# Fewer copies of a bias row in DRAM, low parts of a split operand on one engine, and doubled queries for the first pairs of an attention stage

## What is computed

```
def project(x, W):
    p = rmsnorm(x, W['norm_mix']) @ W['w_in']        # one projection for all head groups
    q, kv, gate, z, xbc, dt_raw = split(p)
    q = rmsnorm(q, W['q_norm'])                      # 8 query heads of 64, 2 KV heads
    ...
bias = rel_bias[rel_bucket(q_pos - k_pos)]           # added to the logits of every branch
def attend_shared(q, q_pos, k, v, k_pos, mask, rel_bias):
    s = einsum('...qgrd,...kgd->...qgrk', q, k) * HEAD_DIM ** -0.5
    p = masked_softmax(s + bias, mask)
    return einsum('...qgrk,...kgd->...qgrd', p, v), p
```

## Time and profile before

| | us |
|---|---|
| median of 3 runs | 2066.74 (2059.92 to 2070.21) |
| profiled execution, its own time | 2045.3 |
| span of its trace | 2043.5 |
| PE busy | 1868.7 (91%) |
| DVE, ACT, POOL busy | 827.5, 741.3, 374.5 |

### The profile page before, as it was taken

One profiled execution on the slowest core, in us unless ns is written; L12 is line 12 of the kernel. 1 busy time (PEld: TensorE's weight loads), 2 busy tenths in 40 slices (PEclk: granted clock), 3 DMA queues, 4 the chain that ended last, 5 costly groups with the idle time before them and its releaser, 6 DMA issues. The chain is left out here.

```text
span 2043.5 us, 31118 instructions
## 1 busy us (share of the span) xinstructions
PE 1868.7 (91%) x11797; PEld 1531.7 (75%) x11797; DVE 827.5 (40%) x1809; ACT 741.3 (36%) x1534; POOL 374.5 (18%) x429
## 2 busy tenths in 40 slices
PE   6879997999988886998986987999999999799899
PEld 5878996666655564655654867999999999587686
DVE  6431266666664573456363442111111211433532
ACT  5222542576664142355352542111111110432422
POOL 5221111343332435325250000000000000000000
PEclk9989997799996897999997998999999999899999
DMA  5543130110000018548394212112111110401300
GB/s 141 83 126 97 42 95 16 40 35 12 12 13 1 1 24 304 170 144 288 124 331 157 75 65 83 41 41 60 43 41 41 50 53 1 134 31 55 119 34 23
DMA packets 155352, 165.93 MB, mean 81 GB/s; under 512 B 45502, under 2 KB 121831, under 8 KB 155178
## 3 DMA queue, kind: packets, MB, share of 16 engines
q1 hardware_dynamic: 136498, 96.81, 16.9%
q0 software_dynamic: 18432, 67.12, 9.4%
q10 hardware_dynamic: 312, 0.52, 0.1%
HBM read 144.37 MB, written 18.47 MB: 80 GB/s over the span
## 5 line engine op out<-in xcount | busy, mean ns | idle before, releaser
L2630 PE MATMUL banks<-u_parts,w_parts 128*128 128x352 f32 x3168 | 505.4, 322 | 8.9 <-DVE w_parts L2644 8.9
L2630 PEld LDWEIGHTS banks<-u_parts,w_parts 128*128 128x128 f32 x3168 | 505.1, 188 | 9.0 <-issue 9.0
L2776 PE MATMUL banks<-w_down_hi,g_parts 128*128 128x512 f32 (+1 forms) x792 | 250.4, 394 | 19.2 <-DVE g_parts L2800 19.2
L467 PE MATMUL banks<-u_parts_mix,w_in_parts 128*128 128x352 f32 x1440 | 246.2, 329 | 21.6 <-ACT columns L631 15.7
L467 PEld LDWEIGHTS banks<-u_parts_mix,w_in_parts 128*128 128x128 f32 x1440 | 232.9, 190 | 25.3 <-ACT columns L631 15.9
L2652 DVE TENSOR_TENSOR gT<-silu_gate,banks 128x352 f32 (+1 forms) x66 | 34.4, 521 | 417.6 <-PE banks L2630 417.6
L2776 PEld LDWEIGHTS banks<-w_down_hi,g_parts 128*128 128x128 f32 (+1 forms) x792 | 142.9, 180 | 63.6 <-DVE w_down_lo_b L2797 20.0
L2800 DVE TENSOR_TENSOR g_parts<-gT,g_parts 128x256 fp32r<-128x256 f32 (+1 forms) x198 | 77.9, 402 | 156.4 <-ACT g_parts L2759 156.4
L2084 ACT ACTIVATE turned<-banks 128x512 f32<-128x512 f32 (+1 forms) x136 | 78.9, 590 | 164.6 <-PE banks L1949 164.1
L1961 PE MATMUL banks<-turned,cmp_w 128*128 128x512 f32 x256 | 134.0, 606 | 4.3 <-DVE turned L2086 2.4
L2759 ACT ACTIVATE g_parts<-gT 128x256 fp32r (+2 forms) x198 | 76.7, 397 | 168.2 <-PE banks L2776 168.2
(11 more groups left out here) (378 smaller groups left out, 2517.3 us busy)
## 6 DMA issues: line engine op xcount, KB each, us to landing
w_raw<-in_w_gate SPq DMA_DIRECT2D x22, 512.0 KB, 4.0
w_raw<-in_w_up SPq DMA_DIRECT2D x22, 512.0 KB, 5.1
w_down_raw<-in_w_down SPq DMA_DIRECT2D x44, 256.0 KB, 3.5
w_in_raw<-in_w_in SPq DMA_DIRECT2D x29, 256.0 KB, 3.5
x_tile<-in_x_prompt SPq DMA_DIRECT2D x8, 512.0 KB, 4.1
x_again<-in_x_prompt SPq DMA_DIRECT2D x8, 512.0 KB, 4.2
w_out_raw<-in_w_out SPq DMA_DIRECT2D x8, 512.0 KB, 7.8
h_dram<-mix SPq DMA_DIRECT2D x8, 512.0 KB, 4.9
```

Source lines behind the costliest of these rows:

```text
L467: mm = nc.tensor.matmul(bank[:, 0:PIECE], w[:, pb, :], u[:, pa, k, tokens(p)], start=(k == 0 and (pa, pb) == TERMS[0]), stop=(k == KT - 1 ...
L2630: mm = nc.tensor.matmul(m.bank[3 * side + q][:, 0:PIECE], wp[:, i, a, k, :], m.u2[:, b, k, q * PIECE:(q + 1) * PIECE], start=(k == 0 and ( ...
L2776: mm = nc.tensor.matmul(m.bank[x.slot][0:x.rows, :], gp[:, g % RG, pa, k, 0:x.rows], part_of(pb, f), start=(f == 0 and (pa, pb) == TERMS[0 ...
```

## The change

There are three edits. The bias rows are copied 16 times a head, and are read back by eight DMAs of 16 partitions. DVE makes the low parts of all token tiles, in a new order with those of block 0, and POOL only those of the weights. Units 0 to 3 of the prompt attention read `q_twice` like the others; its slots 0 and 1 are filled in three steps: heads 0 and 1 before the projection ends, heads 2 and 3 and the slots 2 and 3 at the start of the attention stage. One copy of the compressed keys that nobody reads any more is dropped.

```diff
+BCOPIES = 16
+def double_queries(sp, m, n, rp, half=0):
+    t, g = Q_PAIRS[n]
+    heads = slice(2 * rp, 2 * rp + 2)
+    return sp.dma_start(m.qd[64 * half:64 * half + 64, n % Q_SLOTS, heads, :],
+                        m.qT[64 * g:64 * g + 64, heads, t * P:(t + 1) * P])
...
+    SECOND_Q = blocks.index((NORM, 7, blocks[-3][2]))
-    BY_DVE = 1
...
-                        sp.dma_start(m.bias_dram, m.biasrow[:, :].unsqueeze(1).broadcast_to([NH, P, BIASW])
+                        sp.dma_start(m.bias_dram, m.biasrow[:, :].unsqueeze(1).broadcast_to([NH, BCOPIES, BIASW])
...
-                sp.dma_start(m.bias[:, :, :], bass.AP(m.bias_dram.tensor, 127, [[BIASW - 1, P], [P * BIASW, NH], [1, 256]])
-                             ).then_inc(s.bias_loaded, 16)
+                for p0 in range(0, P, BCOPIES):
+                    sp.dma_start(m.bias[p0:p0 + BCOPIES, :, :],
+                                 bass.AP(m.bias_dram.tensor, 127 - p0, [[BIASW - 1, BCOPIES], [BCOPIES * BIASW, NH], [1, 256]])
+                                 ).then_inc(s.bias_loaded, 16)
+                sp.wait_ge(s.taken_v, taken_before[last_item[SECOND_Q]])
+                for q in range(2):
+                    double_queries(sp, m, q, 0).then_inc(m.q_first, 16)
+                    double_queries(sp, m, q, 0, 1).then_inc(m.q_first, 16)
...
-                sp.wait_ge(s.bias_loaded, 16)
-                sp.wait_ge(s.taken_v, sum(1 for x in by_act if not x))
-                for q in range(2, Q_SLOTS):
-                    t, g = Q_PAIRS[q]
-                    for half in range(2):
-                        sp.dma_start(m.qd[64 * half:64 * half + 64, q, :, :],
-                                     m.qT[64 * g:64 * g + 64, :, t * P:(t + 1) * P]).then_inc(m.q_first, 16)
+                sp.wait_ge(s.bias_loaded, 16 * (P // BCOPIES))
...
-                            if p == 0:
-                                halves_ready(pe, BY_DVE, k // 4)
-                            halves_ready(pe, needs_tile[p], k // 4)
+                            pe.wait_ge(s.u_ready, 2 * needs_tile[p] + k // 4 + 1)
...
-                u_lo(0)
-                u_lo(2)
-                w_lo(1)
-                u_lo(3)
-                w_lo(2)
-                for j in range(4, n):
-                    u_lo(j)
+                for b in range(1, W_RING):
+                    w_lo(b)
...
+                def u_lo(j):
+                    r = slice(j * P, j * P + rows[j])
                     for h in range(2):
                         dve.wait_ge(s.u_hi, 2 * j + h + 1)
+                        nc.vector.tensor_tensor(u[:, LO, 4 * h:4 * h + 4, r], ut_of(j)[:, 4 * h:4 * h + 4, 0:rows[j]],
+                                                u[:, HI, 4 * h:4 * h + 4, r].bitcast(F32), ALU.subtract).then_inc(s.u_ready, 1)
...
-                for j in range(n):
+                make_u(0)
+                scale_x(2)
+                make_u(1)
+                u_lo(0)
+                w_lo_first(0)
+                make_u(2)
+                u_lo(1)
+                w_lo_first(1)
+                u_lo(2)
+                for j in range(3, n):
+                    scale_x(j)
                     make_u(j)
+                    u_lo(j)
...
+                for half in range(2):
+                    for q in range(2):
+                        double_queries(sp, m, q, 1, half).then_inc(s.q_second, 16)
+                for rp in range(2):
+                    for half in range(2):
+                        for q in range(2, QS):
+                            double_queries(sp, m, q, rp, half).then_inc(s.q_third, 16)
...
-                    q = qd[:, (u // 2) % QS, r, :] if u >= 4 else m.qT[:, r, t * P:(t + 1) * P]
-                    if u == 4 and i == 0:
-                        pe.wait_ge(m.q_first, 16 * 2 * (QS - 2))
+                    q = qd[:, (u // 2) % QS, r, :]
+                    if i == 0 and u == 0:
+                        pe.wait_ge(m.q_first, 16 * 4)
+                    if i == 0 and u == 1:
+                        pe.wait_ge(s.q_second, 16 * 4)
+                    if i == 0 and u == 4:
+                        pe.wait_ge(s.q_third, 16 * 8)
...
-                        rows = slice(64 * h, 64 * h + 64) if u >= 4 else slice(64 * g, 64 * g + 64)
+                        rows = slice(64 * h, 64 * h + 64)
```

More of the change, by code:

```diff
@@ L268, in stage_project @@
     n_back = {(b, i): k for k, (b, i) in enumerate([(b, i) for b in backs for i in range(3)])}
-    with stage(nc, "x_loaded*3 raw_landed*3 first_landed*3 w_first w_hi w_ready x_root x_scaled x_turned u_whole u_hi u_ready u_first projected taken_a "
+    with stage(nc, "x_loaded*3 raw_landed*3 first_landed*3 w_first w_hi w_ready x_root x_scaled x_turned u_whole u_hi u_ready projected taken_a "
                    "taken_v squared summed rooted turned_back copied_back stored*2 stored_v kept consts_in rest_in gains_in gains_turned gains_ready warmed pages_in "
@@ L377, in load_compression @@
                         sp.dma_start(w2[:, kv, :], io.cmp_w2[0, kv, :, :]).then_inc(s.w2_loaded, 16)
[L378 removed]
+                    sp.wait_ge(s.u_ready, 2 * n)
                     for half in range(2):
@@ L769, in _ @@
             def _(pool):
-                def u_lo(j):
-                    r = slice(j * P, j * P + rows[j])
-                    ut = ut_of(j)
-                    for h in range(2):
-                        pool.wait_ge(s.u_hi, 2 * j + h + 1)
-                        nc.gpsimd.tensor_tensor(u[:, LO, 4 * h:4 * h + 4, r], ut[:, 4 * h:4 * h + 4, 0:rows[j]],
-                                                u[:, HI, 4 * h:4 * h + 4, r].bitcast(F32), ALU.subtract).then_inc(s.u_ready, 1)
                 def w_lo(b):
@@ L982, in _ @@
                 scale_x(1)
[L983 to L992 removed]
+                make_u(0)
[9 more added lines that the diff above has]
+                    scale_x(j)
+                    make_u(j)
+                    u_lo(j)
+                    if j == 5:
                         dve.wait_ge(s.pages_in, 16)
@@ L1500, in stage_prompt_attention @@
     w = place_compression(nc, m)
-    with stage(nc, "gates_out gates_in tables cmp_loaded q_loaded*4 scored prepared exp_done rated scaled turned copied_v copied_a weighted o_taken dve_c") as s:
+    with stage(nc, "gates_out gates_in tables cmp_loaded q_second q_third q_loaded*4 scored prepared exp_done rated scaled turned copied_v copied_a weighted o_taken dve_c") as s:
         def copied(engine, F):
@@ L1568, in scores @@
                     if branch == 1:
-                        rows = slice(0, 64) if u >= 4 else slice(64 * g, 64 * g + 64)
-                        mm = nc.tensor.matmul(m.bank[2 * (n % 2)][:, 384:384 + cmp_keys(t)], q[rows, :],
-                                              m.kcd[rows, g, 0:cmp_keys(t)], start=True, stop=True)
+                        mm = nc.tensor.matmul(m.bank[2 * (n % 2)][:, 384:384 + cmp_keys(t)], q[0:64, :],
+                                              m.kcd[0:64, g, 0:cmp_keys(t)], start=True, stop=True)
                     mm.then_inc(s.scored, 1)
```

39 lines of the change are left out of this document (9 added, 30 removed).

## The result

| | before | after |
|---|---|---|
| median, timed together | 2063.33 us (2056.06 to 2070.21, 4 runs) | 2040.43 us (2036.08 to 2044.31, 4 runs) |
| profiled execution, span | 2045.3, 2043.5 | 2044.31, 2042.5 |
| PE busy | 1868.7 | 1877.1 |

The ratio is 0.9889, 95% interval 0.9846 to 0.9932: 22.9 us less (14 to 32), 2040.4 us where 2040 was forecast. The two profiled executions, though, are only 1 us apart. Where their difference went is told behind the experiments; first the places of the change.

A forecast was written before the change was run, and what follows sets the result against it. PE idle or at its lower clock in three places (projection, first stage's start, passage and first attention units) was taken as the bound; 17.5 + 0.5 + 2.8 + 5.9 = 26.7 us off 2066.7 gave 2040 us, range 2028 to 2053.

The forecast's parts named there:

- The place of the bound: PE idle or at its lower clock in the projection, at the first stage's start, and at the attention's passage and first units.
- The bias write: Projection: fewer copies let block 6's weights land at about 85.3 us, removing PE's 15.7 us stall and 1.8 us aftermath: 17.5 us.
- a cover of 13: Projection: PE can run on for 13 us while ACT waits for block 6, hiding ACT's remaining 2 us wait.
- The rival that the compression weights hold the load: Projection: block 6's load is late from compression weights, not bias, so 17.5 us are not gained: 2057 us; chance 0.10.
- The bias read: End of projection: eight reads instead of one are hidden before the last norms; cost 0.
- The slower rival: Bias reads use few DMA engines; below 35 GB/s the stage ends late, up to 2097 us; chance 0.03.
- The low parts: First stage: DVE's low parts start the first product 2 us earlier, less three longer waits of 0.7 us: 0.5 us gained.
- The passage: Projection to attention: the stage ends with DVE's last norm, not after SP's query copies; PE starts 2.8 us earlier.
- The doubled queries: Units 0 to 3 of the attention: each of 16 score tiles takes 0.85 us instead of 1.22: 5.9 us.
- The rival of the clock: The clock comes up within units 0 to 3, after about 12 us: 5 us more gain, 2035 us; chance 0.22.
- The sum: Whole kernel: the terms 17.5, 0.5, 2.8 and 5.9 us add up to 26.7 us of gain.
- "The trace can't say where these are": Whole kernel: the timed median lies 21.4 us above the profiled execution, place unknown; the gain is taken as the same there.

The follow-up runs named there:

- copies_64: Changed kernel with 64 copies of the bias rows a head instead of 16, and two reads instead of eight: 2040.24 us, ratio 0.9861 to the kernel before.
- only_bias: Kernel before with 16 copies of the bias rows and eight reads, nothing else: 2028.93 us, ratio 0.9918 to the kernel before.
- copies_128: Changed kernel with the bias edit undone (128 copies, one read of all partitions), other two edits kept: 2062.93 us, ratio 0.9968 to the kernel before.
- after_third: Changed kernel timed and profiled a third time, without an edit: 2011.83 us, ratio 0.9845 to the kernel before.
- only_queries: Kernel before with doubled queries for units 0 to 3 and their copies issued in three steps, nothing else: 2034.93 us, ratio 0.9948 to the kernel before.
- second set: Kernel before (2068.15 us) timed together with copies_64, copies_128 and two other variants of the changed kernel, ratios 0.9838 to 0.9968.
- sets 1 and 2: Timed sets with the kernel before at 2045.77 and 2068.15 us; the first held each edit alone and the change again, the other four variants of the change.

## Why the prediction was right, point by point

The forecast of 2040 us was met to 0.4 us, and that closeness is luck: the median of before had come down by 3.4 us with a fourth run, and the gain was 3.8 us smaller than the 26.7 forecast. What the mechanism is worth is better seen at the start of unit 4, where all three edits are done: the three traces of the change are 26.8, 25.3 and 29.1 us ahead of before's.

- **The place of the bound** was right: all three places gained about what lies there, and the rest of the program kept its times but for the sample attention (below): the stages behind that take 936 to 940 us in the traces of before and of the change.
- **The bias write, 17.5 us**: 16.8 measured alone, and 17.6 at the last norm in its trace. The load came even sooner than the 85.3 us forecast (block 6 is rounded at 82.5 and 83.6), and ACT waited 0.4 us, not 2. The prediction hid those 2 us behind a cover of 13; copies_64 shows that it is 10.5 us, as ACT's and PE's work behind the landing takes the rest. Here nothing hung on it. The rival that the compression weights hold the load is refuted by only_bias. Only copies_128 speaks for more than 17.5 us, and it stays open.
- **The bias read, 0**: nobody waited for it, though it took about 8 us for 5.4. The slower rival, with reads of under 35 GB/s, was off by nearly a factor of four: 1.05 MB in 8 us are 131 GB/s.
- **The low parts, 0.5 us**: the low price holds once POOL is idle, two in 1.29 us. The first product came 1.8 us earlier (1.7 in the mean of all traces, 2 forecast), the three waits grew by 0.3 us each, not by 0.7. That gives 0.9 us, and so do the bias products of all traces: 56.2 us in the mean of the four kernels with the low parts as before, 55.3 in that of the seven with the change's order. The total says 2.3 with an interval of 0.4 to 4.1. By the traces the term was 0.4 us too small: of the 0.5 us allowed for ACT's rounding only 0.1 was needed.
- **The passage, 2.8 us**: 3.15 in the traces, 2.5 in the total.
- **The doubled queries, 5.9 us**: at the lower clock 4.9. The work cut from PE was 6.1 us, close to the forecast, though by two errors that nearly cancel: a tile alone saves 0.42 us, not 0.37 (0.80 for 1.22); but the prediction took a lone tile's price for all 16, and the two tiles that go together in units 2 and 3 save 0.54, 0.27 each. What the prediction had wrong is "with PE busy all through". Before the change PE already waited for ACT 0.79, 0.97 and 0.26 us in units 0 and 1 (the second in the earlier trace rows), 2.0 in sum; after it, with less work between, 1.22, 1.48 and 0.59, 3.3 in sum. So 1.3 us of the cut work are lost. To that comes what the clock gives. The Trainium skill (TensorEngine Tiling (Array Packing), section "Tiling Modes") says that different tiles, two of 64 rows among them, can execute matmuls in parallel, which alone would halve the time at best. The trace agrees in part: 1.22 to 0.80 us is 0.66, 2.07 to 1.53 is 0.74.
- **The rival of the clock** (0.22, 5 us more) was not a rival but part of the case: of the seven traces with doubled queries and no idle matmuls, two have it inside units 0 to 3, worth 1.9 us (after_third) and 4.7 (only_queries); it rose 26 and 16 us behind the first score, not 12. Its premise that PE was busy all through in these units was wrong as well. What the prediction had no means to know is that the same program does it in one execution and not in the next.
- **The sum, 26.7 us**: 22.9, 30.9 and 31.7 us by the ratio, each of its own median of before; 2040.4 us lies in the range of 2028 to 2053 that was given. The last two lie 4 to 5 us above the sum, a little more than their intervals allow; why isn't shown. At the Mamba stage the three traces of the change stand 23.5, 23.4 and 27.2 us ahead of before's, 2 to 3 less than at unit 4, because before's trace has one of the shortest stretches between (299.7 us).
- **"The trace can't say where these are"**, the 21.4 us between the profiled execution and the median. It could have been said only with a second trace. They are in the sample attention. Stretches of an eighth of that stage, the second and the seventh, in the first trace of the change and in after_third:

```profile
801.90:844.90 43.00, 43.00 (x208) 26.04 (x208) 19.60 (x34) 15.68 (x26) 14.67 (x15) 1.00 0.59 193
...
1016.60:1059.60 43.00, 34.72 (x353) 21.26 (x342) 26.27 (x55) 16.91 (x31) 23.31 (x24) 1.00 0.90 288
```

```profile
794.80:834.60 39.80, 39.80 (x195) 24.33 (x194) 17.60 (x30) 14.13 (x24) 14.24 (x14) 1.00 0.60 195
...
994.20:1034.00 39.80, 35.14 (x374) 22.93 (x374) 27.87 (x54) 17.14 (x31) 23.51 (x24) 0.96 0.99 370
```

In the second, PE is busy all through and the rows come at the same rate in both; in the seventh they come at 288 GB/s in the one and at 370 in the other. The stage lasts 343 to 350 us in every trace of the second set and in the first of the change, and 318 to 325.5 in all others. Every long one has waits of 25 us and more in sum that the trace names "remote", such as this one of ACT, and none of the short ones has any:

```profile
ACT turned L2083 <- remote: 24.9, 6, 6.3
```

So the profiled execution of before has the short stage, and the medians of before, 2045.8 and 2044.5 in the sets with the short one and 2068.2 in that with the long one, put its timed runs of 2066.7 with the long one. To compare the two spans, 2043.5 and 2042.5, says nothing of the change. What makes the stage long is open; it goes with the set of runs and not with the kernel, nor with the chip: sets 1 and 2 ran on the same one. It raises the medians of before and of the change alike, so the prediction's step of taking the gain as the same there held within the intervals: 22.9 us (14 to 32) with the long stage, 31 and 32 with the short one.

## What to carry to other kernels

A late transfer costs what it passes the work in hand: find how long its consumer's consumer can go on (here 13 us), take off what must still be done behind the landing (2.6 us), and a wait of that length, 10.5 us, costs nothing; cutting the small rows ahead of it to a half did as well within the noise as to an eighth. Before comparing two traces, compare the length of a stage that the change doesn't touch: here it differed by 20 us, nearly all of the gain. Where PE runs short operations behind a wait, read the granted clock of the stretch; ten small matmuls without use in the waits at a pipeline's start, with 28 ahead of them, were worth 7 us of the first units here.

## What was not expected of the hardware

- The granted clock behind the same wait of 5.8 us came back 16 us (only_queries), 26 us (after_third) or 33 to 34 us (the other five traces with doubled queries and without idle matmuls) behind the first score, with PE's work the same: 2 to 5 us of spread at one place.
- With ten idle matmuls of 128 columns in the first units, and 28 of 352 ahead of them, it didn't fall at all; with the 28 alone it fell 2 to 3 us into the attention in both traces, and came back after 14 us in one and some 30 in the other.
- Two score tiles, each from two 64-row halves of 128 columns, took 1.53 us at 1.2 GHz and one 0.80, where halves of 256 columns took 2.08 for two tiles: half the columns is not half the time.
